# Second mixer: norm weights folded into the projection weights, the rows' roots into the rotation tables and the values

## The reference

```python
def rms_norm(x, g):
    y = xf * lax.rsqrt(jnp.mean(xf * xf, axis=-1, keepdims=True) + NORM_EPS)
    return y * g
h = x
for i in range(DEPTH):                       # 2
    hn = rms_norm(h, norm_mix[i])
    if i % 2 == 0: h = h + short_conv_mixer(hn, conv_w_in, conv_w, conv_w_out)
    else:          h = h + dilated_attention_mixer(hn, w_qkv, w_o, cos, sin)
    h = h + hierarchical_moe(rms_norm(h, norm_ffn[i]), ...)
return rms_norm(h, norm_final)
# attention: qkv = (x @ w_qkv) split into 3 groups x (q, k, v); q and k are turned by
# t1*cos - t2*sin, t2*cos + t1*sin; v is used as it is
```

## Time and profile before

| | us |
|---|---|
| median of 3 runs | 1478.22 |
| lowest, highest | 1478.21, 1480.15 |
| the profiled execution | 1483.25 |
| its span, first to last instruction | 1481.5 |
| PE busy in it | 1370.3 (92%) |
| DVE, ACT, POOL busy | 986.5, 760.5, 222.4 |
| mean granted clock of TensorE | 0.966 |

### The profile page before, as it was taken

How to read it: one execution, slowest core, us unless ns; L and a number is a source line. 1 busy time by engine, 2 the same in 40 slices (tenths; PEclk the granted TensorE clock), 3 DMA queues, 4 the chain that set the end, 5 groups by cost and what they waited for, 6 DMA issues and landing times.

```text
span 1481.5 us, 20812 instructions
## 1 busy us (share of the span) xinstructions
PE 1370.3 (92%) x7335; PEld 1134.1 (77%) x7335; DVE 986.5 (67%) x1179; ACT 760.5 (51%) x843; POOL 222.4 (15%) x313
## 2 busy tenths in 40 slices
PE   4999977999999959999998999999889699999994
PEld 4888766888888848888877888887767588888883
DVE  6445367999999974342548434344855799999997
ACT  4222244878888732423256142224713478888882
POOL 4000021111111321120200111120002111111123
PEclk9999987999999969999999999999999699999997
DMA  6237426999999942232210222231023699999993
GB/s 216 85 100 311 170 89 232 376 386 389 393 395 389 349 181 87 84 114 85 86 58 2 86 85 86 90 110 58 2 86 142 222 369 388 397 381 391 386 348 136
DMA packets 85105, 308.93 MB, mean 209 GB/s; under 512 B 11905, under 2 KB 11929, under 8 KB 68660
## 3 DMA queue, kind: packets, MB, share of 16 engines
q1 hardware_dynamic: 76404, 292.26, 53.0%
q0 software_dynamic: 8640, 15.86, 2.8%
HBM read 292.24 MB, written 31.46 MB: 218 GB/s over the span
## 4 chain that ended last, share of the span: by engine, by line
PE 85%; DVE 8%; issue 3%; ACT 2%; DMA 1%; SPq 1%; DVEq 0%; POOLq 0%; ACTq 0%
PE ps L312 25%; PE ps L314 25%; PE ps L313 25%; PE ps L1749 2%; DVE h L1195 1%; PE ps L1564 1%; DVE probT L1360 1%; PE ps L1799 1%; PE ps L1703 1%; PE ps L1735 1%; DMA x_rows<-hn_rows,tok_list 1%; DVE hn L980 1%; ACT prob L844 1%; ACT W_hi L715 1%; PE ps L1579 1%
## 5 line engine op out<-in xcount | busy, mean ns | idle before, releaser
L312 PE MATMUL ps<-W_hi,xT_hi_all 128*128 128x512 f32 x1408 | 560.1, 398 | 6.6 <-DVE xT_lo_all L1393 4.5
L314 PE MATMUL ps<-W_hi,xT_lo_all 128*128 128x512 f32 x1408 | 551.9, 392 | 0.0
L313 PE MATMUL ps<-W_lo,xT_hi_all 128*128 128x512 f32 x1408 | 550.7, 391 | 0.0
L1124 DVE TENSOR_TENSOR W_lo<-m_raw,W_hi 128x2048 fp32r<-128x2048 f32 x192 | 435.9, 2291 | 58.9 <-ACT W_hi L715 57.0
L715 ACT ACTIVATE W_hi<-m_raw 128x2048 fp32r<-128x2048 f32 x192 | 367.0, 1914 | 48.3 <-PE ps L314 47.9
L935 DVE TENSOR_TENSOR W_lo<-raw,W_hi 128x2048 fp32r<-128x2048 f32 x56 | 135.3, 2416 | 277.7 <-ACT W_hi L663 277.6
L312 PEld LDWEIGHTS ps<-W_hi,xT_hi_all 128*128 128x128 f32 x1408 | 266.0, 189 | 64.6 <-DVE xT_lo_all L1393 4.8
L314 PEld LDWEIGHTS ps<-W_hi,xT_lo_all 128*128 128x128 f32 x1408 | 265.8, 189 | 57.5
L313 PEld LDWEIGHTS ps<-W_lo,xT_hi_all 128*128 128x128 f32 x1408 | 266.3, 189 | 51.9
L663 ACT ACTIVATE W_hi<-raw 128x2048 fp32r<-128x2048 f32 x56 | 107.1, 1913 | 367.6 <-PE ps L314 364.9
L630 POOL TENSOR_TENSOR qk_rot<-rope_a,rope_b 128x512 f32<-128x512 f32 x48 | 61.8, 1292 | 395.0 <-DVE rope_b L1422 394.9
(11 more groups left out here) (230 smaller groups left out, 1415.0 us busy)
## 6 DMA issues: line engine op xcount, KB each, us to landing
m_raw<-in_w_gate_dram SPq DMA_DIRECT2D x64, 1024.0 KB, 7.7
m_raw<-in_w_up_dram SPq DMA_DIRECT2D x64, 1024.0 KB, 8.8
m_raw<-in_w_down_dram SPq DMA_DIRECT2D x64, 1024.0 KB, 7.8
raw<-in_attn_w_qkv_dram SPq DMA_DIRECT2D x36, 1024.0 KB, 5.1
raw<-in_conv_w_in_dram SPq DMA_DIRECT2D x12, 1024.0 KB, 5.1
y_rows<-zero_rows SPq DMA_DIRECT2D x2, 4096.0 KB, 17.3
y_pick<-y_rows SPq DMA_DIRECT2D x16, 512.0 KB, 7.0
raw<-in_conv_w_out_dram SPq DMA_DIRECT2D x4, 1024.0 KB, 5.9
```

Source lines behind the costliest of these rows:

```text
L312: pe.matmul(o, a_hi, b_hi, start=first, stop=False)
L313: pe.matmul(o, a_hi, b_lo, start=False, stop=False)
L314: return pe.matmul(o, a_lo, b_hi, start=False, stop=last)
L1124: dve.tensor_tensor(MW_lo[c % MSPLIT][:, :, :], m_raw[c % MRAW][:, :, :], MW_hi[c % MSPLIT][:, :, :].bitcast(F), ALU.subtract).then_inc(s[ ...
```

## The change

**Norm weights.** For the units 16 to 51 (`normed`) `hi` becomes four ACT copies of 128x512, one per slice `k` of the contraction, with a scale from the new tile `mix_gain`, and `lo` four DVE instructions `scalar_tensor_tensor` of the same size (raw x scale - high). `mix_gain` is loaded at the program's start, by a new transfer of 4 KB on SP's queue ahead of `conv_rows`, the router weights and the first weight units. The 512 KB load of the second mixer's norm weights to `gain` goes away, with `norm_row` and `turn_rows` of this stage.

**Root.** DVE multiplies `cos_t` and `sin_t` by `rstd` once, and the copies of the values take `rstd` as their scale.

**Rows.** PE transposes `h` itself, row tile by row tile as it becomes ready. The first 512 columns of q go by row tile and not by unit: `first_chunk` takes (row tile, half) in the order (0,0), (0,1), (1,0), (1,1), (2,0), (3,0), (2,1), (3,1), with the transposes of tiles 1, 2 and 3 between them. The two units are on the chip before: the load of unit 16 stands ahead of `y_back` in SP's queue, and ACT makes its high part within `experts(0)`.

**Row tile 1 of the stored results** is added by DVE too, in both layers: `scaled_rows` on POOL and the ACT scaling are gone. The written order of DVE is `first_rows` for layer 0 and `last_layer_rows` for layer 1.

```diff
@@ SyncE @@
             sp.dma_start(pos_i[:, :], pos_v).then_inc(pos_in, 16)
+            sp.dma_start(mix_gain[:, :], norm_mix[1].rearrange("(p k) -> p k", k=KD)).then_inc(mix_gain_in, 16)
...
-            norm_gain(2)
             sp.wait_ge(zeroed, 32)
             later_weights(0)
+            qkv_unit(0, 0, 0)
             y_back(0)
-            for j in range(3):
+            for j in range(1, 3):
                 qkv_unit(j, 0, 0)
@@ ScalarE @@
+                if normed(uc, rev):
+                    act.wait_ge(mix_gain_in, 16)
+                    for k in range(4):
+                        ins = act.activation(W_hi[uc % SPLIT][:, k, :], raw[uc % RAW][:, k, :], ACT.Copy,
+                                             scale=mix_gain[:, 4 * (uc % 2) + k:4 * (uc % 2) + k + 1])
...
-                act.wait_ge(s["pick_in"][1], 32)
-                for c in range(2):
-                    act.activation(y_pick[2 + c][:, :], y_pick[2 + c][:, :], ACT.Copy, scale=gates[:, c, 1:2]
-                                   ).then_inc(s["scaled"], 1)
+                if l == 0:
+                    hi(U_QKV)
                 last_split(1, later * 6 + 5, slice(3, 5))
...
+            turn_hi(2, 0)
+            hi(U_QKV + 1)
             square(0, 8, h_ready, 4 + 1)
+            for r in range(1, NT):
+                turn_hi(2, r)
+                square(r, 8, h_ready, 4 + r + 1)
+            act.wait_ge(rstd_ready, 12)
@@ VectorE @@
+                    for k in range(4):
+                        ins = dve.scalar_tensor_tensor(
+                            out=W_lo[uc % SPLIT][:, k, :], in0=raw[uc % RAW][:, k, :],
+                            scalar=mix_gain[:, 4 * (uc % 2) + k:4 * (uc % 2) + k + 1],
+                            in1=W_hi[uc % SPLIT][:, k, :].bitcast(F), op0=ALU.mult, op1=ALU.subtract)
...
+            def first_rows():
+                after(stored_rows(0, 0, 0))
+                after(stored_rows(0, 0, 1))
+                after(stored_rows(0, 1, 0))
+                last_split(0, 1, slice(3, 5))
+                after(stored_rows(0, 1, 1))
+                last_rows(0, 0)
+                lo(U_QKV)
+                turn_lo(2, 0)
+                last_rows(0, 1)
+                lo(U_QKV + 1)
...
+                turn_lo(2, 2)
+                turn_lo(2, 3)
+                dve.wait_ge(rstd_ready, 12)
+                dve.tensor_tensor(cos_t[:, :, :], cos_t[:, :, :], bc(rstd[:, :], HD), ALU.mult)
+                after(dve.tensor_tensor(sin_t[:, :, :], sin_t[:, :, :], bc(rstd[:, :], HD), ALU.mult))
@@ TensorE @@
+            def first_chunk():
+                for r, kh in ((0, 0), (0, 1), (1, 0), (1, 1), (2, 0), (3, 0), (2, 1), (3, 1)):
+                    if r == 0:
+                        pe.wait_ge(split_lo, RAW + U_QKV + kh + 1)
+                    if kh == 0:
+                        pe.wait_ge(v_ready, r + 1)
+                        pe.wait_ge(x_lo, 8 + r + 1)
+                    for k in range(4):
+                        ...
+                    if r == NT - 1:
+                        ins.then_inc(unit_done, 1)
+                    elif kh == 1:
+                        ins.then_inc(qkv_done, 1)
+                    if (r, kh) in ((0, 0), (1, 0)):
+                        turn_row(4, r + 1)
+                    if (r, kh) == (1, 1):
+                        turn_row(4, 3)
```

More of the change, by code:

```diff
@@ L645, in _ @@
             moe_rows(0)
-            scaled_rows(0)
             rstd_tiles(8)
@@ new lines, in last_layer_rows @@
+            def last_layer_rows():
+                after(stored_rows(1, 0, 0))
+                after(stored_rows(1, 0, 1))
+                after(stored_rows(1, 1, 0))
+                last_split(1, 1, slice(3, 5))
+                after(stored_rows(1, 1, 1))
+                last_rows(1, 0)
+                last_rows(1, 1)
+                after(stored_rows(1, 2, 0))
+                after(stored_rows(1, 2, 1))
+                norm_row(3, 16, 0)
+                last_rows(1, 2)
+                after(stored_rows(1, 3, 0))
+                norm_row(3, 16, 1)
+                after(stored_rows(1, 3, 1))
+                last_rows(1, 3)
+                norm_row(3, 16, 2)
+                norm_row(3, 16, 3)
@@ L1649, in experts @@
                 place_last(0, 1)
-                for r in range(1, 3):
-                    place_last(r, 0)
-                    place_last(r, 1)
+                place_last(1, 0)
+                place_last(1, 1)
+                if l == 0:
+                    turn_row(4, 0)
+                place_last(2, 0)
+                place_last(2, 1)
                 place_last(3, 1)
@@ L1773, in _ @@
                     for p in range(3):
-                        for kh in range(2):
+                        for kh in range(2 if s + g + p else 0):
                             uc, ui = U_QKV + 2 * p + kh, s * 18 + g * 6
```

121 lines of the change are left out of this document (50 added, 71 removed).

## The result

The changed kernel takes about 1.5% less time, and its time is inside the range given (1450.5 to 1460.5), but not at its middle.

A forecast was written before the change was run, and what follows sets the result against it. PE bounds the kernel almost everywhere, losing time in waits for DVE and at low clock between layer 0 and unit 18 and at the end. -20.5 - 5.2 + 0.55 = -25.2 gives a median of 1453.0 us, range 1450.5 to 1460.5.

The forecast's parts named there:

- Part 1: From layer 0's experts to unit 18: fewer PE waits on DVE start unit 18 at 554.9 instead of 575.4, -20.5 us.
- wait of 0.3 for unit 17's low part: In the first chunk of q products, PE waits once, 0.3 us, for unit 17's low part; chunk ends at 553.4.
- The durations without a row: Splitting units in 512-column pieces: DVE 0.75 us each, 2.76 for four overlapped; ACT 2.5 for four.
- Rival B: Split pieces cost as much as 1024 elements; unit 18 starts at 563.7, time 1461.9 us; chance 0.15, whole or half.
- The new wait: Ahead of unit 18, PE waits about 1.4 us for ACT's split, DVE's low part, then the rotation freeing bank 0.
- Part 2: Program's end, where DVE is the chain: adds no longer slowed and norms reordered, last norm at 1471.2, -5.2 us.
- Part 3: Costs: +0.55 us for a small load at the start; later units, value scales, router weights and picks nothing.
- +0.55 of the small load: At the start, one more small transfer on SP's queue ahead of the first weights: +0.55 us (0.4 to 0.9).
- The sum: Whole kernel: -20.5 - 5.2 + 0.55 = -25.2 us, taking the profiled execution from 1483.25 to 1458.1.
- the step to the median: Profiled execution lies 5.0 us above the median of 1478.22, so the new median becomes 1453.0 us.
- All forecast idles: PE's new idles, 1.1, 0.3 and 1.4 us in the hand-over and 0.9 at the end, keep full clock.
- rival A: Short idles drop the clock at the second `last_lo` of both layers; +4.8, time 1457.9 us; chance 0.15.

The follow-up runs named there:

- e2: Kernel before, with DVE adding row tile 1 of the stored results in both layers, without ACT's scaling and POOL's adding of it: 1473.12 us, ratio 0.9947.
- e3: Changed kernel with the old end of layer 1 (ACT scales and POOL adds row tile 1, one norm in its old place): 1462.26 us.
- e4: Changed kernel with the first 512 columns of q taken unit by unit, a transposed row tile between the products: 1467.44 us.
- e6: Changed kernel with the rotation of row tiles 0 and 1 ahead of unit 18's low part and the `mix_gain` load later: 1459.05 us.
- e8: Changed kernel with two useless DVE instructions ahead of the second `last_split` of layer 0, lengthening PE's idle: 1464.12 us.
- e7: Changed kernel with one useless DVE instruction ahead of the second `last_split` of layer 0, lengthening PE's idle: 1461.69 us.

## Why the prediction was right, and where it was off

**Direction and mechanism: right.** The gains of parts 1 and 2 were found where the prediction put them: POOL's share by e2 and e3, the order by row tile by e4, the folding as what is left between the two.

**Part 1: -20.5 forecast, -19.65 found** against the same execution. The forecast times have to be moved by the 2.04 us by which this execution reached the first `last_lo` earlier. Then the second one-hot block was forecast at 520.7 and started at 520.71. The first product: 527.0, found 527.31. The end of the first chunk: 551.4, found 552.07 (551.84 and one distance). Unit 18: 552.9, found 553.71. The 0.85 us missing are many small ones: one-hot matmuls start 0.233 apart and not 0.2267, the products of the first chunk 0.2287, the first distance behind an idle is 0.34 and behind transposes 0.31 to 0.34, and one of the three blocks of transposes between products costs 0.91 where I took 0.80. In the other direction, the wait of 0.3 for unit 17's low part did not come. None of these had been visible as a row that I used; they should have been an item of half a microsecond.

**The durations without a row: right.** The line between 384 and 1024 elements gave 0.75 for a 512-element piece on DVE; all 144 have a mean of 754 ns, four together take 2.74 (forecast 2.76). ACT's pieces have a mean of 712 ns, four 2.55 (2.5). Rival B is out.

**The new wait: right.** 1.4 forecast, 1.48 found, on `rope_b`, through the chain that was named: ACT's part, DVE's part, then the rotation. The one cheap way out of it that was tried, e6, does not work.

**Part 2: -5.2 forecast, -4.92 found** against the same execution. Its price depends on the execution of the kernel before: against the mean of five profiles it is 26.72 - 22.97 = 3.75.

**Part 3: not settled.** The +0.55 of the small load is not to be seen in one pair: the first product came at 23.95, against 24.40 before. Over all profiles with the load at the start (6) it comes at 23.73 in the mean (22.59 to 25.04), over those without it (7) at 23.27 (22.25 to 24.52). The difference of 0.46 fits the forecast and is smaller than the scatter; e6, with the load moved away, came at 24.52, late and not early. The later units, the values' scale, the router's weights and the picks cost nothing that a row shows; from unit 18 to the attention PE waits for nothing new.

**The sum was right, the step to the median failed.** "The profiled execution, 1483.25 (span 1481.5), would be 1458.1 (1456.3)": it was 1458.0 (1456.3). That it agrees to 0.1 us is in part luck. The two stretches of the forecast gave 24.4 us and not 25.7; start and middle, which scatter, gave 0.9 in this pair, where the forecast had taken 0.55 off. Between the means of all profiles the gain is 23.2, as worked out below. Then came "it lies 5.0 above the median of 1478.22, so the median becomes 1453.0", and this step failed, for two reasons. First, the three times shown were low ones: 52 runs have a median of 1481.96, and the profiled execution lies only 1.3 above it. Second, the 5 us were not an offset that a change leaves alone. Most of the kernel before's scatter comes from its long idles: behind them the clock is low for 5 to 13 matmuls, and once it did not fall at all. The change removes these idles, and with them most of the scatter (12 us wide over 52 runs before, 2.8 over 9 after). The time of the kernel after is then better taken from the walk through one execution, as an absolute time, than from the gain subtracted from another median; here that would have been 1458.1, for a median of 1458.37 over all runs.

By means over all profiles the account reads: hand-over 243.95 to 223.25, -20.7; end 26.72 to 22.97, -3.75; together -24.45. Against this stand +0.4 to the first `last_lo` (514.67 in five profiles of the kernel before, 515.10 in seven of the changed one and its variants, e6 without the early load among them) and +0.8 in the middle (690.0 and 690.8). That makes -23.2, and the medians of all runs differ by 23.6. The +0.4 has the size of the small load, but it is smaller than the scatter and not shown to be that. The +0.8 is the clock: matmuls are slow at two places of layer 1 that the change does not touch (near 1080 and 1150 us). Over all 13 profiles the middle takes 689.3 to 689.6 us with 13 slow ones there, 690.3 to 690.4 with 17, and 690.7 to 691.3 with 19 to 23. One profile of a changed variant, e8, has 13, and its middle of 689.6 is that of the kernel before: so the new splits and scaled copies cost nothing there. Why most profiles with the change have 19 and more stayed open; the idle ahead of the first place is 4.53 us in all of them.

**The clock.** All forecast idles kept it: 0.87 and 1.48 us, with a granted clock of 1.00 around them. But the ground was thinner than I wrote. I read "idle for 2.2 us or more when it fell" out of mean clocks over stretches; in e7 an idle of 2.19 was enough, and the clock fell behind it. Had the second `last_lo` come 1.3 us later, rival A would have been true in this layer, at about two thirds of its price. And no single length divides the two cases: e4 kept the clock through idles of 2.46, 2.54 and 3.48 us. What else decides is open. The rule of the Trainium skill's page "TensorE: Matmul & The Clock Gate", section "Part 4: PE-mode transpose", that transposes do not count as matmuls do, had no effect here: three blocks of them between products, 0.8 to 0.9 us each, left the granted clock at 1.00 from 527.3 to 551.9. In e4 each block stood together with an idle, 3.50 to 4.52 us from the first transpose to the next product, and the clock stayed at 1.00 too. No run has a longer row of transposes at full clock, so the rule itself is not tested further.

**DVE beside POOL.** What the rows showed as 2.9 against 1.3 us for an addition, e2 and e3 confirm by taking POOL's additions away and putting them back (3.91 for three, 6.17 for two). The Trainium skill's page "SBUF — State Buffer", section "SBUF: two separate sides", describes a port pair that the two engines lock against each other for a whole instruction, when VectorE's has two inputs in SBUF and GpSimd's reads SBUF, as both do here. The measured durations go the way of that rule, in e6 too; no run tests it against another reason for the slowing.

## What to carry to other kernels

If a change removes the cause of a kernel's scatter, forecast the absolute time from the walk through one execution, and do not subtract the gain from a median of a few runs. Where PE stands idle for about two microseconds or more, a delay on another engine can cost about twice itself (1.3 us more idle cost 2.8 in e7, 2.65 cost 5.1 in e8), so look first for what slows that engine, such as additions on GpSimd beside it. But do not count on a length: in e4 idles of 2.5 to 3.5 us cost only themselves. Between transposes and the product that needs them, other products should stand as cover: this order alone was worth 7 us, nearly as much as the 8.7 of folding the norm away with all that goes with it.

## What the runs showed of the hardware beyond what was expected

- Idles of TensorE of 0.87, 1.48 and 1.78 us left the matmuls behind them fast (0.23 apart); behind idles of 2.19, 2.58, 2.85, 3.14 and 3.52 us they started 0.43 apart; behind idles of 2.46, 2.54 and 3.48 us, each after a block of transposes in e4, they were fast again. So the length alone does not tell.
- The clock can be lost behind an idle and not in it: in e7 it was 1.00 over the idle of 2.19 us and over the first 0.24 us of the next matmul, and 0.50 after that.
- How soon the full clock returns varies for one and the same program: behind the idle ahead of the second one-hot block of layer 0 after 5, 6 or 13 matmuls.
- Two additions of 128x1024 f32 on VectorE beside two on GpSimd took 4.76 to 6.37 us over the profiles of one program; alone they take 2.61. Four pieces of 128x512 took 2.74 alone and 3.77 beside GpSimd's additions.
